# Down projections computed slab by slab over both column chunks, five of 22 k-pairs with seven block products, and a ninth gate/up chunk likewise

## The reference: what is computed

```python
def swiglu(x, w_gate, w_up, w_down):
    return (jax.nn.silu(x @ w_gate) * (x @ w_up)) @ w_down
...
    h = layer_norm(DEEPNORM_ALPHA * h + 0.5 * swiglu(h, ffn1_w_gate[l], ffn1_w_up[l], ffn1_w_down[l]), ln1_g[l], ln1_b[l])
    mix = hybrid_mixer(...)
    h = layer_norm(DEEPNORM_ALPHA * h + mix, ln2_g[l], ln2_b[l])
    h = layer_norm(DEEPNORM_ALPHA * h + 0.5 * swiglu(h, ffn2_w_gate[l], ffn2_w_up[l], ffn2_w_down[l]), ln3_g[l], ln3_b[l])
```

## Time and profile before

| what | value |
|---|---|
| time of 3 runs | 2691.24 us median (2691.07 to 2692.39) |
| profiled execution | 2690.13 us, span of its instructions 2688.5 us |
| granted TensorE clock, mean | 0.995 |
| PE busy | 2653.2 us (99%), 12624 matmuls |
| DVE busy | 1844.9 us (69%) |
| ACT busy | 1314.2 us (49%) |
| HBM traffic | 191 GB/s over the span |

### The profile page before, as it was taken

One profiled execution on the slowest core, in us unless ns is written; L12 is line 12 of the kernel. 1 busy time (PEld: TensorE's weight loads), 2 busy tenths in 40 slices (PEclk: granted clock), 3 DMA queues, 4 the chain that ended last, 5 costly groups with the idle time before them and its releaser, 6 DMA issues.

```text
span 2688.5 us, 36549 instructions
## 1 busy us (share of the span) xinstructions
PE 2653.2 (99%) x12624; PEld 2205.5 (82%) x12624; DVE 1844.9 (69%) x2170; ACT 1314.2 (49%) x1610; POOL 128.0 (5%) x168
## 2 busy tenths in 40 slices
PE   8999999999999999999999999999999999999997
PEld 6888888888787788888888888888878888888886
DVE  6999994545576665677777765444689999845555
ACT  4555554433344454555655554444355555544333
POOL 1000000000000000221111100000000000000000
PEclk9999999999999999999999999999999999999999
DMA  6666666666555545665655565657566666657654
GB/s 207 203 193 206 195 197 193 223 194 194 181 182 146 148 152 196 205 181 181 182 176 176 179 181 166 190 192 245 196 199 200 196 198 199 200 187 256 226 191 138
DMA packets 285659, 514.08 MB, mean 191 GB/s; under 512 B 19616, under 2 KB 52560, under 8 KB 282992
## 3 DMA queue, kind: packets, MB, share of 16 engines
q1 hardware_dynamic: 279552, 485.03, 57.5%
q0 software_dynamic: 4336, 25.36, 2.6%
q10 hardware_dynamic: 1664, 2.26, 0.2%
HBM read 506.23 MB, written 6.36 MB: 191 GB/s over the span
## 4 chain that ended last, share of the span: by engine, by line
PE 97%; DVE 2%; ACT 0%; issue 0%; DMA 0%; POOL 0%; POOLq 0%; SPq 0%; ACTq 0%; DVEq 0%
PE acc L749 19%; PE acc L751 19%; PE acc L750 19%; PE acc L815 5%; PE acc L817 5%; PE acc L816 5%; PE spare L816 4%; PE spare L817 4%; PE spare L815 4%; PE spare L718 2%; PE spare L834 1%; PE acc L834 1%; PE acc L835 1%; PE spare L833 1%; PE acc L833 1%; PE spare L835 1%
## 5 line engine op out<-in xcount | busy, mean ns | idle before, releaser
L1610 DVE TENSOR_TENSOR w_lo<-land,w_hi 128x1024 fp32r<-128x1024 f32 (+1 forms) x956 | 1155.7, 1223 | 686.3 <-ACT w_hi L1216 678.9
L1216 ACT ACTIVATE w_hi<-land 128x1024 fp32r<-128x1024 f32 (+1 forms) x956 | 976.1, 1028 | 983.0 <-PE acc L751 590.7
L749 PE MATMUL acc<-w_hi,a_hi 128*128 128x512 f32 (+1 forms) x1184 | 451.5, 381 | 2.6 <-DVE a_lo L1657 1.8
L751 PE MATMUL acc<-w_hi,a_lo 128*128 128x512 f32 (+1 forms) x1184 | 436.0, 368 | 0.0
L750 PE MATMUL acc<-w_lo,a_hi 128*128 128x512 f32 (+1 forms) x1184 | 434.7, 367 | 0.0
L749 PE MATMUL acc<-w_hi,g_hi 128*128 128x512 f32 x680 | 264.9, 390 | 0.0
L750 PE MATMUL acc<-w_lo,g_hi 128*128 128x512 f32 x680 | 264.7, 389 | 0.0
L751 PE MATMUL acc<-w_hi,g_lo 128*128 128x512 f32 x680 | 264.7, 389 | 0.0
L749 PEld LDWEIGHTS acc<-w_hi,a_hi 128*128 128x128 f32 x1184 | 224.1, 189 | 46.7 <-issue 9.2
L751 PEld LDWEIGHTS acc<-w_hi,a_lo 128*128 128x128 f32 x1184 | 223.8, 189 | 38.2
L750 PEld LDWEIGHTS acc<-w_lo,a_hi 128*128 128x128 f32 x1184 | 224.3, 189 | 37.2 <-issue 3.6
(11 more groups left out here) (333 smaller groups left out, 3493.1 us busy)
## 6 DMA issues: line engine op xcount, KB each, us to landing
land<-w_in SPq DMA_DIRECT2D x232, 512.0 KB, 3.9
land<-ffn_w_gate SPq DMA_DIRECT2D x176, 512.0 KB, 3.8
land<-ffn_w_up SPq DMA_DIRECT2D x176, 512.0 KB, 4.5
land<-ffn_w_down SPq DMA_DIRECT2D x176, 512.0 KB, 4.2
land<-w_ssd_o SPq DMA_DIRECT2D x64, 512.0 KB, 4.4
land<-w_in SPq DMA_DIRECT2D x132, 128.0 KB, 2.3
land<-w_attn_o SPq DMA_DIRECT2D x32, 512.0 KB, 4.1
land<-w_out SPq DMA_DIRECT2D x32, 512.0 KB, 4.3
```

The costliest lines, as they stand in the source:

```text
L749: pe.matmul(to, rows_hi, hi, start=first, stop=False)
L751: mm = pe.matmul(to, rows_lo, hi, start=False, stop=last)
L1216: act.activation(w_hi[:, l % SPLIT, 0:deep, 0:width], land[:, l % LAND, 0:deep, 0:width], ACT.Copy).then_inc(high, 1)
L1610: dve.tensor_tensor(w_lo[:, l % SPLIT, 0:deep, 0:width], land[:, l % LAND, 0:deep, 0:width], w_hi[:, l % SPLIT, 0:deep, 0:width].bitcast(F ...
```

## The change

Three things change. (1) `NC_S` goes from 8 to 9: chunk 9 of gate and up takes seven products in the same three k-pairs. (2) In `down` both column chunks of a pass go side by side: the slabs of one k-pair for the left and the right chunk follow each other, into four banks `own`. Five k-pairs (11, 13, 15, 17, 19) of each pass take seven block products, with the other four banks as `aux`. In the first pass the k-pairs come in natural order, in the second the five are moved forward. The combined rows for the five come from `g_hi`, `g_lo` and are formed by DVE and ACT in the first pass (`mixed_down`, `mixed_high`, `mixed_low`), between slabs 11 and 21. DVE folds the shared products in once for each pass (`collect_down`), and the scaling of the residual moves to slabs 10 to 16 of the first pass. (3) In chunk 0 the combined rows for gate and up are formed with `mixed_high` one slab later on ACT and `mixed_low` one slab later on DVE. To make the residual ready earlier POOL reloads its right half in chunk 10 and its left half after the last turn; the rows of gain and bias are loaded between the two. Addresses of some buffers change, and the semaphore counts with them.

```diff
-NC_S = 8
+NC_S = 9
+DOWN_SEVEN = (11, 13, 15, 17, 19)
+DOWN_ORDER = (tuple(range(22)), (0, 1, 2, 3, 11, 4, 13, 5, 15, 6, 17, 7, 19, 8, 9, 10, 12, 14, 16, 18, 20, 21))
+DOWN_SLABS = ([(p, c) for p in range(22) for c in range(2)],
+              [(p, c) for p in range(18) for c in range(2)] + [(p, c) for c in range(2) for p in range(18, 22)])
...
+            def down(f):
+                for j in range(2):
+                    own, aux = chunk_banks(1 - j), chunk_banks(j)
+                    if j == 0:
+                        pe.wait_ge(gt_out, 2 * chunk_no(f, NC_F - 1))
+                    else:
+                        pe.wait_ge(aux_out, shared_down(f, 0) + 1)
+                    for l, (p, c) in enumerate(DOWN_SLABS[j]):
+                        if j == 1 and l >= 44 - HALVED:
+                            break
+                        if j == 0 and l == 3:
+                            turn_hidden(f, NC_F - 1, (NC_F - 1) % 2)
+                        s = DOWN_ORDER[j][p]
+                        if s in DOWN_SEVEN:
...
+                            if c == 0:
+                                down_seven_block(f, j, l, own, aux)
+                        else:
+                            down_slab(f, j, l, own).then_inc(used, 1)
...
             def up_first(f, ln, cols):
...
-                    if l >= 16 - 2 * len(SEVEN) and l % 2 == 0:
-                        mixed_high(f, (l - 16) // 2 + len(SEVEN))
+                    if l > 16 - 2 * len(SEVEN) and l % 2 == 1:
+                        mixed_high(f, (l - 17) // 2 + len(SEVEN))
...
+            def collect_down(f, j):
+                aux = chunk_banks(j)
+                one, late, both = d_parts[:, 0, :], d_parts[:, 1, :], d_parts[:, 2, :]
+                left, right = (resid[:, :, (2 * j + c) * W:(2 * j + c + 1) * W] for c in range(2))
+                dve.wait_ge(q_copied, shared_down(f, j) + 1)
+                ch.link(dve.tensor_tensor(both, one, aux[:, 3, :], ALU.add))
+                ch.link(dve.tensor_tensor(late, both, aux[:, 2, :], ALU.add))
+                ch.link(dve.scalar_tensor_tensor(out=left, in0=d_parts[:, 0:2, :], scalar=0.5, in1=left,
+                                                 op0=ALU.mult, op1=ALU.add))
+                dve.tensor_tensor(d_parts[:, 1:3, :], aux[:, 1:2, :].to_broadcast([P, TOK, W]), d_parts[:, 1:3, :],
+                                  ALU.subtract).then_inc(aux_out, 1)
...
             def down(f):
                 phase = f"down{f}"
                 for j in range(2):
-                    for l in range(44):
+                    for l, (p, c) in enumerate(DOWN_SLABS[j]):
+                        s = DOWN_ORDER[j][p]
...
-                        if l in (18, 36):
-                            c = 2 * j + l // 36
+                        if j == 0 and l in (10, 12, 14, 16):
+                            at = (2, 3, 0, 1)[(l - 10) // 2]
+                            part = resid[:, :, at * W:(at + 1) * W]
                             if f == 1:
...
                                 ch.link(dve.tensor_scalar(part, part, ALPHA, None, ALU.mult))
                             else:
-                                prepare_rows(2, c)
+                                prepare_rows(2, at)
+                        if j == 0 and l in (11, 13, 15, 17, 19, 21):
+                            q = (l - 11) // 2
+                            if q > 0:
+                                mixed_low(f, len(SEVEN) + q - 1)
+                            if q < len(DOWN_SEVEN):
+                                mixed_down(f, q)
+                        if (j, l) == (1, 0):
+                            collect_down(f, 0)
+                        if j == 1 and l in (3, 4):
+                            evacuate_down(f, 0, l - 3)
+                        if (j, l) == (1, 30):
+                            collect_down(f, 1)
...
                         split(phase, j, l)
+                        if n is not None and c == 1:
+                            t_low_parts(n, "down")
+                evacuate_down(f, 1, 0)
```

More of the change, by code:

```diff
@@ new lines, in down_slab @@
+            def down_slab(f, j, l, banks, tiles=range(TOK)):
+                phase = f"down{f}"
+                p, c = DOWN_SLABS[j][l]
+                s = DOWN_ORDER[j][p]
+                pe.wait_ge(rest, slab_no(phase, j, l) + 1)
+                for k in range(2):
+                    for t in tiles:
+                        to = banks[:, 2 * c + t, :]
+                        rows_hi = g_hi[:, 2 * s + k, t * P:(t + 1) * P]
+                        rows_lo = g_lo[:, 2 * s + k, t * P:(t + 1) * P]
+                        hi, lo = w_hi[:, l % SPLIT, k, :], w_lo[:, l % SPLIT, k, :]
+                        mm = three(to, (rows_hi, rows_lo), (hi, lo), p == 0 and k == 0, p == 21 and k == 1)
+                return mm
@@ L935, in ffn @@
                     up_plain(f, i)
[L936 to L946 removed]
+                down(f)
             pe.wait_ge(p_seq, 2)
@@ L1695, in evacuate_half @@
                 else:
-                    acc_ready(phase, i, cc)
-                moved = dve.scalar_tensor_tensor(out=part, in0=acc[:, 2 * pair + t, :], scalar=scale, in1=part,
+                    dve.wait_ge(used, slab_no(phase, i, sum(n for n, _ in PHASES[phase][1]) - 1) + 1)
+                moved = dve.scalar_tensor_tensor(out=part, in0=acc[:, 2 + t, :], scalar=scale, in1=part,
                                                  op0=ALU.mult, op1=ALU.add)
@@ L1867, in up_seven @@
                     split(f"up{f}", i, l)
                     if l // 2 in SEVEN and l % 2 == 1:
-                        t_low_parts(seven_block(f, i, l // 2))
+                        t_low_parts(seven_block(f, i, l // 2), "up")
+            def collect_down(f, j):
[9 more added lines that the diff above has]
+                                  ALU.subtract).then_inc(aux_out, 1)
+                dve.wait_ge(aux_out, shared_down(f, j) + 1)
+                for t, part in enumerate((both, late)):
+                    ch.link(dve.scalar_tensor_tensor(out=right[:, t, :], in0=part, scalar=0.5, in1=right[:, t, :],
+                                                     op0=ALU.mult, op1=ALU.add))
@@ new lines, in evacuate_down @@
+            def evacuate_down(f, j, c):
+                phase = f"down{f}"
+                last = max(l for l, (_, cc) in enumerate(DOWN_SLABS[j]) if cc == c)
+                dve.wait_ge(used, slab_no(phase, j, last) + 1)
+                part = resid[:, :, (2 * j + c) * W:(2 * j + c + 1) * W]
+                dve.scalar_tensor_tensor(out=part, in0=chunk_banks(1 - j)[:, 2 * c:2 * c + 2, :], scalar=0.5, in1=part,
+                                         op0=ALU.mult, op1=ALU.add).then_inc(down_out, 1)
+                dve.wait_ge(down_out, (f - 1) * 4 + 2 * j + c + 1)
+                ch.link(statistics(2 * j + c))
```

263 lines of the change are left out of this document (175 added, 88 removed).

## The result

| | before | after |
|---|---|---|
| median of 4 runs each | 2691.15 us (2691.05 to 2692.39) | 2669.45 us (2668.99 to 2670.97) |
| profiled execution | 2690.13 us | 2668.99 us |
| span of its instructions | 2688.5 us | 2667.4 us |
| matmuls | 12624 | 12546 |

The ratio is 0.9921, with a 95% interval of 0.9907 to 0.9935: faster by 0.8%, 21.7 us. Forecast were 2669.3 us in a range of 2666.0 to 2677.0.

A forecast was written before the change was run, and what follows sets the result against it. PE was taken as the bound. Matmuls removed, chunk 0's wait and DVE's lateness in down gave -17.7 - 5.3 + 1.0 = -22.0 us; against the median 2669.2, stated as 2669.3 us, range 2666.0 to 2677.0.

The forecast's parts named there:

- Term 1: Down stages and chunk 9: 78 matmuls fewer on PE at 0.2267 us each, 17.7 us gained.
- Term 2: Chunk 0: new order removes PE's wait at slab 10 and slow clock behind it, 5.3 us back (bounds 0 and 5.7).
- Term 3: Added DVE work in down: slab 17 of the second block's first pass 1.0 us late, pairs cost nothing (0 to 4.7).
- The covers: Row loads, `collect_down` at the pass turn and last evacuation with statistics cost nothing: cover 9, 6 and 1.8 us.
- A: Chunk 0's wait stays or returns at slabs 11 to 14: 2672.5 to 2674.6 us; chance 0.12.
- B: DVE falls further behind in down's preparation: 4.7 us, up to 3 more at pairs, 2673 to 2676; chance 0.15.
- C: Turn of a down pass not covered, PE waits for `collect_down` in both blocks: 13.5 us, 2683; chance 0.03.
- D: DVE can't keep pace at the 20 seven-product down pairs, so slower: 2705 us at 12 us per two k-pairs; chance 0.03.
- point of decision: DVE's time for two k-pairs in down: 10.2 us costs nothing, 11.3 loses the whole gain, from 11.6 slower by over 0.2%.

The follow-up runs named there:

- run 4: Kernel after with NC_S = 8 instead of 9, so chunk 9 of gate and up is plain again; 2674.01 us.
- run 1: Kernel before with only the new order of combined rows in chunk 0 (ACT and DVE one slab later); 2685.42 us against 2691.09.
- run 2: Kernel after with the old order of combined rows in chunk 0; 2675.93 us.
- run 3: Kernel after with the residual's quarters prepared at slabs 8 to 14 of the first down pass instead of 10 to 16; 2668.58 us.
- run 7: Kernel after with two unused DVE operations added at each seven-product down pair and `last_rows` loaded only after slab 36 of that pass; 2671.32 us.
- run 5: Kernel after with two unused DVE operations (1.45 us together) added at each of the 20 seven-product down pairs; 2676.39 us.

## Why the prediction was right, step by step

**Term 1** (17.7 us) was exact: 6.80 us per down stage and 2.04 per chunk 9, measured in both blocks apart, and the chunk again by run 4. The Trainium skill (TensorE: Matmul & The Clock Gate, on the 56 ns gap) would have made 6.47 of the 6.80 with its 215.7 ns, as an estimate; the measurement decides for the distance in the trace.

**Term 2** (5.3 us) measured 4.9 in the kernel after and 5.1 by run 1. Its working was off in three places. The table load was counted on the path and is not: it goes ahead of the wait for PE, so that the SiLU started 1.2 us earlier than worked out and slab 10's high part ended at 37.5, not 38.7. That changed nothing in the time, since DVE is the later of the two, as forecast (its low part ends at 40.63, worked out 40.5). For the same reason the rule by which 0.7 us of the gain would go (the Trainium skill, ScalarE: Activation LUTs, on the cost of the table load) had nothing to act on here. And the short waits that remain were put at 0.3 us, at slab 14 alone; at slabs 12 and 14 together they cost about 0.9, since each matmul is recorded 0.16 us longer than the distance to the next, which the record of an idle time leaves out, and the start behind a wait is 0.34 instead of 0.23 us from the next. The measured 4.9 lies within the bounds. But the upper one, 5.7, took the tax of the slow clock (1.7) from the one execution at hand: with the same wait it is 2.9 in run 2, which puts the order at 5.9 although the short waits are still in it.

**Term 3** (1.0 us) measured 1.26, at the slab named, on the operand named, 0.2 us later than worked out; run 3 took it away. That the first block has none of it was right too (0.07). Behind it the working has a slip: PE's first pair is put at 61.7 + 1.0, but 0.9 + 22 x 2.72 is 60.7, so the 1.0 stands in it twice. The lead at that pair is then 4.6 us where 4.05 are needed, 0.5 to spare and not 1.5. The first sum came 57.15 us into the stage (forecast 57.1), and by the measure given with run 7 the lead there is 0.35 us (6.29 against 5.94). That cost nothing in the kernel as it is, and it fits that run 7 loses time in this pass and in no other.

**The covers** held. At the end of the stage DVE has 2.07 us before the half evacuation, forecast 1.8; the kernel after there, for the earlier trace rows:

```profile
2644.68 1.29 DVE L1781 BATCH_NORM_STATS2 stats<-resid 128x6 f32<-128x512 f32 x2
2648.03 0.69 DVE L1824 SCALAR_TENSOR_TENSOR resid<-acc,resid 128x512 f32<-128x512 f32 x1 [2.07 <-PE acc L873]
```

`collect_down` never held PE at the turn of a pass. One cover was not counted, since the load of `last_rows` was taken as POOL's old business: it falls beside the new `collect_down` on DVE at slab 30 and leaves PE in the kernel as it is without a wait, but with 1.45 us a pair more on DVE its place costs 5 to 6 us (runs 5 and 7).

**The rivals.** *A* (the wait in chunk 0 comes back at slab 11 to 14) came true in small: 0.9 us at slabs 12 and 14. *B* (the preparation, 4.7 us) stayed at 1.26. *C* (the turn of a pass) showed nothing. *D* (DVE can't hold the pace of the pairs) has its point of decision where it was put: DVE's need is 9.08 us (forecast 9.3), and at 10.53 the three passes with a lead still show nothing (run 7). At 11.98 the kernel is at 2702 us, where 2705 stood for 12; that closeness is in part luck, since 2705 counts 1.8 us at each of the 20 pairs, the leads save some 8 of these 36, and the wait beside `last_rows` adds 5.

## What to carry to other kernels

Price work on the bounding engine by the distance between starts in the trace, then check each supplier by its period against that engine's period and by the lead that it has when the dense stretch begins: a supplier whose period is a little too long shows every tenth of it where it has no lead, and one with a lead hides the deficit for a few rounds and then pays in full. List every transfer that runs in the stretch that gets new work, also those that the change leaves alone: a cover that holds now can be used up by a delay that was harmless before. And after a wait of some microseconds on TensorE, leave a range for the slow clock behind it, rather than the value of one execution.

## What the runs showed of the hardware

- The same wait of 3.8 us on TensorE was followed by some 8 matmuls at the 1.2 GHz level in the kernel before (tax 1.7 us) and by 13 in run 2 (2.9 us). In slab 0, at PE's start, it was none to nine over the twelve kernels traced. No run here tells what decides between them.
- A recorded idle time of 0.32 us on TensorE was 0.48 us of distance lost between the two starts, and about 0.6 with the slower start behind it.
- A 512 KB load of weights issued beside a 2 MB load of broadcast rows landed after 10.54 us in run 5, after 9.7 to 10.2 in the kernel after and after 6.4 to 9.9 in the kernel before (median of all such weight loads in the kernel after 4.7).
